# Constant-table products on TensorE ahead of its waits for each norm and for the route

## The reference

```python
x = layer_norm(ALPHA * x + mixer(x), ln1_g[l], ln1_b[l])
x = layer_norm(ALPHA * x + moe(x),   ln2_g[l], ln2_b[l])
```

## Time and profile before

| what | value |
|---|---|
| median of 3 runs | 2536.15 us |
| profiled execution | 2540.94 us |
| its span | 2538.9 us |
| mean granted TensorE clock | 0.933 |
| PE busy | 2254.6 us (89%) |
| PEld busy | 1694.7 us (67%) |
| DVE busy | 1114.8 us (44%) |
| ACT busy | 752.8 us (30%) |
| POOL busy | 139.3 us (5%) |

### The profile page before, as it was taken

The page is one execution under the profiler, slowest core; times in us unless marked ns, Lnnn a source line. Parts: engine busy times, 40 slices in busy tenths (PEclk is TensorE's granted clock), DMA queues, the critical chain, the costliest instruction groups (busy, mean ns, idle before and its releaser), DMA issues. The chain is left out here.

```text
span 2538.9 us, 32283 instructions
## 1 busy us (share of the span) xinstructions
PE 2254.6 (89%) x13426; PEld 1694.7 (67%) x13426; DVE 1114.8 (44%) x1586; ACT 752.8 (30%) x1154; POOL 139.3 (5%) x114
## 2 busy tenths in 40 slices
PE   7977999999787869999998799877999999777998
PEld 7864454444276844444443799877998999767997
DVE  4562112111167731111212555566555555666555
ACT  3431111111133221111110344444443444453443
POOL 0010000000012210000000000021000000031000
PEclk9988999999986779999999899888999999888999
DMA  9336999999941259999999655522454556423551
GB/s 294 118 130 240 416 420 421 420 420 420 384 147 49 69 222 416 420 420 420 420 421 405 208 176 174 166 88 96 167 198 166 185 171 208 134 67 100 179 171 66
DMA packets 231549, 622.79 MB, mean 245 GB/s; under 512 B 15456, under 2 KB 166944, under 8 KB 182112
## 3 DMA queue, kind: packets, MB, share of 16 engines
q1 hardware_dynamic: 225952, 604.99, 63.0%
q0 software_dynamic: 3040, 10.78, 1.3%
q10 hardware_dynamic: 2400, 4.83, 0.5%
HBM read 619.51 MB, written 1.05 MB: 244 GB/s over the span
## 5 line engine op out<-in xcount | busy, mean ns | idle before, releaser
L425 DVE TENSOR_TENSOR w_low<-ring,w_high 128x1024 fp32r<-128x1024 f32 x380 | 463.0, 1232 | 396.3 <-ACT w_high L418 396.3
L226 PE MATMUL bank<-xT_high,w_high 128*128 128x256 f32 x1712 | 495.0, 289 | 21.4 <-DVE xT_low L477 13.3
L418 ACT ACTIVATE w_high<-ring 128x1024 fp32r<-128x1024 f32 x380 | 393.5, 1052 | 351.3 <-PE bank L226 321.5
L226 PE MATMUL bank<-xT_low,w_high 128*128 128x256 f32 x1712 | 492.2, 287 | 0.0
L226 PE MATMUL bank<-xT_high,w_low 128*128 128x256 f32 x1712 | 491.5, 287 | 0.0
L1289 PE MATMUL bank<-ring,arena 128*64 128x512 f32 x1792 | 451.5, 593 | 36.7 <-DMA w_parts<-in_moe_w_up 14.6
L1289 PEld LDWEIGHTS bank<-ring,arena 128*64 128x64 f32 x1792 | 147.4, 137 | 330.2 <-issue 330.1
L226 PEld LDWEIGHTS bank<-xT_high,w_high 128*128 128x128 f32 x1712 | 336.7, 197 | 29.0 <-DVE xT_low L477 14.4
L1289 PE MATMUL bank<-w_parts,arena 128*64 128x512 f32 x1024 | 346.0, 603 | 1.7 <-issue 1.7
L226 PEld LDWEIGHTS bank<-xT_low,w_high 128*128 128x128 f32 x1712 | 336.9, 197 | 3.1
L226 PEld LDWEIGHTS bank<-xT_high,w_low 128*128 128x128 f32 x1712 | 336.4, 196 | 0.0
(11 more groups left out here) (262 smaller groups left out, 2738.9 us busy)
## 6 DMA issues: line engine op xcount, KB each, us to landing
ring<-in_moe_w_gate SPq DMA_DIRECT2D x128, 1024.0 KB, 18.5
ring<-in_moe_w_up SPq DMA_DIRECT2D x96, 1024.0 KB, 21.1
w_parts<-in_moe_w_down SPq DMA_DIRECT2D x96, 1024.0 KB, 15.3
ring<-in_ffn_gate SPq DMA_DIRECT2D x44, 1024.0 KB, 6.2
ring<-in_ffn_up SPq DMA_DIRECT2D x44, 1024.0 KB, 5.6
ring<-in_ffn_down SPq DMA_DIRECT2D x44, 1024.0 KB, 5.5
w_parts<-in_moe_w_up SPq DMA_DIRECT2D x32, 1024.0 KB, 23.3
arena<-in_moe_w_down SPq DMA_DIRECT2D x32, 1024.0 KB, 17.1
```

Of the source, the lines that this page charges most:

```text
L226: ins = e.matmul(out, lhs, rhs, start=first and i == 0, stop=last and i == len(parts) - 1)
L418: e.activation(hi, src, ACT.Copy).then_inc(*S.high.tell(key))
L425: e.tensor_tensor(lo, src, hi.bitcast(F32), ALU.subtract).then_inc(*S.low.tell(key))
```

## The change

A new helper issues products of the identity with 512 columns of `scan`. They write the bank that the next real work is going to overwrite, and nobody reads them. They are issued behind the bank's own wait and ahead of the wait for the norm, or for the route. Every product is plain float32. In `transpose_x_pe` their number depends on what came before the norm and on the block of tokens; in `route_pe` it is five.

```diff
+def busy_pe(e, k, bank, count):
+    for _ in range(count):
+        e.matmul(bank[:, :], k.ident, k.busy_columns, start=True, stop=True)
+
+BUSY = {"mixer": (2, 3), "experts": (5, 3), "ffn": (3, 4)}
+
-def transpose_x_pe(e, k, n):
+def transpose_x_pe(e, k, n, after=None):
...
             view = pairs(k.banks.open(e, B_BANKS, ("xT", n, tb, half))[:, :], 4)
+            if n >= 0 and half == 0:
+                busy_pe(e, k, k.banks["xT", n, tb, half], BUSY[after][tb])
             if n >= 0:
                 e.wait_ge(*S.x_tok[n, tb])
...
-    view = k.banks.open(e, A_BANKS, ("places", layer))[:, 0:3 * N_EXPERTS].rearrange("p (a b) -> p a b", a=3)
+    bank = k.banks.open(e, A_BANKS, ("places", layer))
+    busy_pe(e, k, bank, 5)
+    view = bank[:, 0:3 * N_EXPERTS].rearrange("p (a b) -> p a b", a=3)
     earlier, ones = k.tab("earlier"), k.tab("ones")
     e.wait_ge(*S.route_step["chosen", layer])
...
+    k.busy_columns = k.tables[:, cols["scan"][0]:cols["scan"][0] + BANK]
...
-        transpose_x_pe(e, k, 0)
+        transpose_x_pe(e, k, 0, "mixer")
...
-        transpose_x_pe(e, k, 1)
+        transpose_x_pe(e, k, 1, "experts")
...
-            transpose_x_pe(e, k, n + 1)
+            transpose_x_pe(e, k, n + 1, "ffn")
```

More of the change, by code:

```diff
@@ L2499, in pe_program @@
     elif part == 1:
-        transpose_x_pe(e, k, 1)
+        transpose_x_pe(e, k, 1, "experts")
         od_pe(e, k, 1)
-        transpose_x_pe(e, k, 2)
+        transpose_x_pe(e, k, 2, "mixer")
         route_pe(e, k, 1, 2)
@@ L2505, in pe_program @@
     else:
-        transpose_x_pe(e, k, 3)
+        transpose_x_pe(e, k, 3, "experts")
         for layer in range(DEPTH):
@@ L2509, in pe_program @@
             ffn_pe(e, k, 2 * layer, n)
-            transpose_x_pe(e, k, n + 1)
+            transpose_x_pe(e, k, n + 1, "ffn")
             hgrn_pe(e, k, layer, n + 1)
-            transpose_x_pe(e, k, n + 2)
+            transpose_x_pe(e, k, n + 2, "mixer")
             ffn_pe(e, k, 2 * layer + 1, n + 2)
             if layer + 1 < DEPTH:
-                transpose_x_pe(e, k, n + 3)
+                transpose_x_pe(e, k, n + 3, "ffn")
 def act_program(e, k, part):
```

## The result

The changed kernel took 2526.53 us, the median of 6 runs (2521.86 to 2528.19), against 2538.12 us of the kernel before (6 runs, 2535.77 to 2542.84). The ratio is 0.9945, with a 95% interval from 0.9932 to 0.9957: 11.6 us faster, where 11 were forecast. A second, later measurement of the same kernel gave 0.9936 (0.9919 to 0.9953). The profiled execution took 2521.86 us with a span of 2519.8 us and a mean clock of 0.957, against 0.933 before. It is the fastest of the six runs, and 4.55 us of the difference had arisen ahead of the first table product, as the next rows show. That part is not the change's: from 60 to 80 us the granted clock was 1.00 in this execution and 0.80 in the one before, in the same program.

A forecast was written before the change was run, and what follows sets the result against it. TensorE and the chains between engines were taken to bound the kernel outside the experts, weights inside. Gains 4.6 + 5.7 + 1.1 + 0.5 = 11.9 us, nine tenths about 11, took median 2536.15 to 2525 us; range 2513 to 2540.

The forecast's parts named there:

- The gain is the clock: At the norms: the products end no wait; anything won is won behind the waits, in TensorE's clock.
- Price of a product: One added float32 product of 512 columns: 0.9 us at the full clock, 1.75 us at the low one, an estimate.
- They fit: Full-clock products fit the waits: mixers 1.8 in 1.89 us, 2.7 in 3.20; feed-forwards 2.7 in 2.82, 3.6 in 3.88.
- Norms behind the experts: First transposes 2 us late, first dense product within 0.5 us; norm 1 wins 1.1 us, norm 3 0.5 us.
- (a): At the seven norms other than 1 and 3, second transposes take 1.29 instead of 1.95 us: 4.6 us.
- (b): Dense products behind the same seven norms cost 0.093 us less each: 11.3 us, of which half, 5.7 us, was taken.
- rival 2: Clock falls again ahead of dense products, 3.3 us or more without work if transposes hold nothing; median 2533; chance 0.20.
- Nine tenths reach the end: Of the 11.9 us summed at the norms, nine tenths reach the kernel's end: 10.7 us, about 11 us.
- The route's five are worth nothing: In the route: five products fit the 9.14 us wait, the places' ten instructions stay slow; nothing counted.
- Rival 1: All of (b) comes, with 2 us in the routes: 21.5 us, median 2515; chance 0.10.
- rival 3: Added products run at the low clock and delay the norms' transposes: 20 to 28 us slower, median 2560; chance 0.12.

The follow-up runs named there:

- the last gap filled: The changed kernel with one more product at each norm, behind the second transposes and ahead of the first dense product: 2521.33 us, ratio 0.992 to the kernel before.
- the run with two more: The changed kernel with two more unread products at each of the 18 places at the norms: 2535.86 us, ratio 0.9984 to the kernel before.

## Why the prediction was right

The time (2525 forecast, 2526.53 measured) and the mechanism were right. That 11 us forecast and 11.6 us measured agree so closely is partly luck: one term was too small by 2 us or more, and the later measurement of the same kernel gave some 16 us. Step by step:

- *The gain is the clock.* Shown by the stretches behind the norms (0.50 before, 1.00 at six of nine after), by the last gap filled, which takes away the slow products that were left and about 6 us with them, and by the run with half of the rows, where only the rows differ.
- *Price of a product.* Taken as 0.9 and 1.75 us; it is 0.86 us at the full clock, the lower bound. At norm 1 four instructions, two products, took 3.44 us at the low clock, so 1.7 us each.
- *They fit.* Yes at mixers and feed-forwards, where each group of transposes starts 0.06 us behind the scale of its norm.
- *Norms behind the experts.* The first transposes were forecast 2 us late; they came 1.07 us late at norm 1 and 2.85 us at norm 3. TensorE was taken to start with DVE; it did in this profile, at 690.56 beside 690.93, but in the run with nine products in the route it was 4.6 us behind at norm 3. The slack that was to absorb the rest was there.
- *(a)* 0.65 us at each of seven norms: 3.45 - 2.81 = 0.64.
- *(b)* The mis-sized term. I let half of the slow products go, 80 left of 160, because the idle stretch of 1.5 us stays open. Counted in the timelines, five profiled executions with whole table products (or their transposes) at every norm and the last gap open left 48 (twice), 60, 63 and 75, and one left 73 without those behind the experts, where 44 of them lie behind norms 1 and 3. At 59 the gain is 101 x 0.093 = 9.4 us instead of the 7.3 us in the sum. The clock was lost at three to five of the nine norms in these profiles. The transposes keep the clock too, so the stretch without work is 1.5 us and not the 3.3 us of rival 2.
- *Nine tenths reach the end.* Not separated from the noise: (a) and (b) in the new sizes give 13.9 us, and the measured gains are 11.6 us and 16 us. In the two profiled executions, with 48 slow products, they give 4.5 + 112 x 0.093 = 14.9 us, and 19.1 - 4.55 = 14.6 us arose from norm 0 on.
- *The route's five are worth nothing.* Shown, to about 1 us (ratio 1.0005, 0.9996 to 1.0013).
- *Rival 1* (no slow dense products left) came true only in kernels that fill more than the change does, *rival 2*'s rule on transposes fell, and *rival 3*'s price was real (the run with two more pays it), though half of the rows did not bring its full loss.

What stays open: what the 1 us per route is worth, whether the products behind the experts give more than their intervals, and why the clock is lost behind one norm and held behind the next with the same idle stretch.

## What to carry to other kernels

Where the first dense products behind a wait run at a granted clock of 0.50, work that nobody reads can hold the clock, and it costs nothing as long as it ends ahead of the signal. Size it by the full clock and check that the real instruction still has its own wait in the timeline. What does not fit is paid, unless another engine's work hides it, as DVE's did behind the experts. Then look for the last idle stretch ahead of the dense work: here 1.5 us of it, left open, cost three to five of nine norms their clock, and one product of 0.86 us at each norm was worth some 4 to 6 us.

## What the runs showed of the hardware

- Products of 64 rows held a full clock through both waits of a mixer's norm, and did not raise a low one in 17 us without a gap, eight of them with two groups of transposes among them. Products of 128 rows raised it at the same place some 4 us after they began, and in other runs 3 to 6 us after. The products were of an identity and a table of ones; no run used other data in their place.
- Float32 transposes of 128x128 hold and raise the clock like products (ratio 0.994 against 0.9936 to 0.9945).
- A float32 product of 512 columns is two instructions 0.43 us apart at the full clock, and 0.86 us at the low one (3.44 us for four).
- A group of transposes that waits for VectorE's signal started 0.06 us behind it where products stood just ahead, and 0.15 us where TensorE had only waited, at either clock.
